# Feed-forward weights by two units in one DMA: 8 KB from each partition in place of 4 KB

## The reference

```
D_MODEL, SEQ, DEPTH, D_FF = 1024, 256, 2, 2816
# first_block, at the end of each of its 2 layers i
hn = rms_norm(h, norm_ffn[i])
gu = hn @ w_gate_up[i]                                  # 1024 x 5632
h = h + (jax.nn.silu(gu[..., :D_FF]) * gu[..., D_FF:]) @ w_down[i]
# second_block
cs = jax.nn.silu(c)
mod = cs @ w_ada[l] + b_ada[l]                          # w_ada: 1024 x 6144
# peer_ffn: rows of two tables of 16384 x 1024 by index
u = expert_u[idx]
v = expert_v[idx]
```

## Time and profile before

| | us |
|---|---|
| median of 3 timed runs | 1472.59 |
| lowest and highest | 1466.71, 1474.99 |
| the profiled execution's own time | 1478.32 |
| its span | 1476.7 |
| TensorE busy | 1384.1 (94%) |
| DVE busy | 1151.5 (78%) |
| ScalarE busy | 761.3 (52%) |
| GpSimd busy | 499.6 (34%) |

### The profile page before, as it was taken

One profiled execution on the slowest core, in us unless ns is written; L12 is line 12 of the kernel. 1 busy time (PEld: TensorE's weight loads), 2 busy tenths in 40 slices (PEclk: granted clock), 3 DMA queues, 4 the chain that ended last, 5 costly groups with the idle time before them and its releaser, 6 DMA issues.

```text
span 1476.7 us, 25782 instructions
## 1 busy us (share of the span) xinstructions
PE 1384.1 (94%) x8444; PEld 1072.0 (73%) x8444; DVE 1151.5 (78%) x2775; ACT 761.3 (52%) x1774; POOL 499.6 (34%) x600
## 2 busy tenths in 40 slices
PE   9999999999999899999999989989999988888888
PEld 9888999999889899998998985444454433333333
DVE  7767788778868688668799778877887888787764
ACT  6646444456556344456885544444444454444433
POOL 1011111110110111011110025766767666667672
PEclk9999999999999999999999999999999999999999
DMA  9999999999999999999999858999999999999997
GB/s 349 342 345 338 372 407 394 382 389 340 319 335 353 396 360 400 393 392 355 341 325 332 327 185 320 389 391 376 409 407 403 400 411 409 396 389 410 403 408 312
DMA packets 141598, 542.73 MB, mean 368 GB/s; under 512 B 22654, under 2 KB 22798, under 8 KB 128064
## 3 DMA queue, kind: packets, MB, share of 16 engines
q0 software_dynamic: 101904, 396.41, 72.3%
q1 hardware_dynamic: 39024, 142.44, 25.4%
q10 hardware_dynamic: 576, 2.72, 0.5%
HBM read 576.08 MB, written 135.27 MB: 482 GB/s over the span
## 4 chain that ended last, share of the span: by engine, by line
PE 53%; DMA 23%; DVE 11%; issue 5%; ACT 4%; POOL 3%; POOLq 0%; DVEq 0%; ACTq 0%; SPq 0%
DMA late<-expert_uv,idx 9%; PE PS L742 8%; PE PS L759 8%; PE PS L750 8%; PE PS L1263 7%; DMA attn<-expert_uv,idx 7%; DMA ada<-w_ada 6%; PE PS L893 3%; PE PS L790 3%; PE PS L1002 2%; PE PS L1006 2%; PE PS L1007 2%; DVE late L2563 2%; PE PS L1219 2%; DVE attn L2563 2%
## 5 line engine op out<-in xcount | busy, mean ns | idle before, releaser
L1366 ACT ACTIVATE early_splits<-ring 128x1024 fp32r<-128x1024 f32 x166 | 175.3, 1057 | 123.0 <-PE PS L750 87.5
L1825 DVE TENSOR_TENSOR early_splits<-ring,early_splits 128x1024 fp32r<-128x1024 f32 x166 | 202.6, 1221 | 33.5 <-ACT early_splits L1366 33.4
L2563 DVE CUSTOM_DVE_ANT_0 late<-late,PS 128x1024 f32<-128x1024 f32 x125 | 152.0, 1216 | 63.7 <-DMA late<-expert_uv,idx 63.0
L1727 ACT ACTIVATE gel<-dot 128x1 f32<-128x1 f32 x256 | 51.7, 202 | 278.7 <-DVE dot L2563 278.0
L2563 DVE CUSTOM_DVE_ANT_0 attn<-attn,PS 128x1024 f32<-128x1024 f32 x125 | 151.9, 1215 | 35.8 <-DMA attn<-expert_uv,idx 30.4
L1263 PE MATMUL PS<-late,wrg 128*128 128x512 f32 x284 | 136.4, 609 | 17.9 <-ACT wrg L1720 17.9
L1263 PE MATMUL PS<-attn,wrg 128*128 128x512 f32 x288 | 134.9, 601 | 7.4 <-ACT wrg L1720 6.5
L1300 PE MATMUL PS<-late,wrg 128*128 128x512 f32 x208 | 104.1, 626 | 31.2 <-ACT wrg L1720 31.2
L674 POOL DMA_INDIRECT attn<-expert_u,idx x93 | 87.8, 944 | 102.8 <-DVE idx L2515 74.7
L684 POOL DMA_INDIRECT attn<-expert_v,idx_v x93 | 93.0, 1000 | 78.2 <-DVE idx_v L2577 30.4
L1263 PEld LDWEIGHTS PS<-late,wrg 128*128 128x128 f32 x284 | 52.1, 193 | 86.9 <-issue 86.8
(11 more groups left out here) (458 smaller groups left out, 3379.7 us busy)
## 6 DMA issues: line engine op xcount, KB each, us to landing
ring<-wstream SPq DMA_DIRECT2D x257, 512.0 KB, 9.5
expert_uv<-expert_u POOLq DMA_DIRECT2D x64, 1024.0 KB, 14.4
expert_uv<-expert_v POOLq DMA_DIRECT2D x64, 1024.0 KB, 16.3
ada<-w_ada POOLq DMA_DIRECT2D x32, 512.0 KB, 13.5
late<-w_ada POOLq DMA_DIRECT2D x16, 512.0 KB, 14.9
late<-wstream SPq DMA_DIRECT2D x4, 512.0 KB, 8.8
attn<-expert_u,idx POOLq DMA_INDIRECT x93, 8.4
attn<-expert_v,idx_v POOLq DMA_INDIRECT x93, 7.7
```

The lines of the kernel that those rows point to most:

```text
L1366: act.activation(hi_of(u), raw(u), ACT.Copy).then_inc(hi_ready, 1)
L1825: ve.tensor_tensor(lo_of(u), raw(u), hi_of(u).bitcast(F32), ALU.subtract).then_inc(units_begun, 1)
L2563: ve.tensor_tensor_reduce(row, row, H2N[n // 8], 1.0, 0.0, ALU.mult, ALU.add, dot[:, n % 2, k:k + 1]).then_inc(dot_ready, 1)
```

## The change

Of the 66 feed-forward units of a layer, the 64 from an even one on (34 to 97 and 132 to 195) are loaded by twos. One DMA takes both units of a pair, 8 KB from each partition, into two neighbouring slots of the ring, and adds 16 to the semaphore of the even slot alone. It waits until both slots are free. The first and the last feed-forward unit of each layer (33 and 98, 131 and 196) and all other units are loaded as before. Who waits for an odd unit of a pair waits for the even slot's semaphore; the counts of the odd slots' semaphores leave the pairs out. The layout in memory is the same.

```
+PAIRED_FROM = [34, 132]
+PAIRED = 64
+        def paired(u):
+            return any(at <= u < at + PAIRED for at in PAIRED_FROM)
+        def landed(u):
+            if paired(u):
+                u -= u % 2
+            if u % 2:
+                return unit_landed[u % RING], 16 * sum(not paired(v) for v in range(u % RING, u + 1, RING))
+            return unit_landed[u % RING], 16 * (u // RING + 1)
@@ SyncE
+            def load_pair(u, i=None):
+                src = wstream[u // DMAU] if i is None else wstream[bass.ds(i * (RING // DMAU) + u // DMAU, 1)].rearrange(
+                    "o p e -> (o p) e")
+                sp.dma_start(ring[:, (u % RING) * D:(u % RING + 2) * D], src).then_inc(unit_landed[u % RING], 16)
-                with sp.Fori(0, 3 * NF // RING) as i:
-                    for m in range(RING):
-                        sp.wait_ge(units_begun, i * RING + (at + m - RING + 1))
-                        load(at + m, at + m, i)
+                for u in range(at, PAIRED_FROM[layer]):
+                    sp.wait_ge(units_begun, u - RING + 1)
+                    load(u, u)
+                at = PAIRED_FROM[layer]
+                with sp.Fori(0, PAIRED // RING) as i:
+                    for m in range(0, RING, 2):
+                        sp.wait_ge(units_begun, i * RING + (at + m - RING + 2))
+                        load_pair(at + m, i)
+                for u in range(at + PAIRED // RING * RING, at + PAIRED, 2):
+                    sp.wait_ge(units_begun, u - RING + 2)
+                    load_pair(u)
+                for u in range(at + PAIRED, LAYER_AT[layer] + PROJ_UNITS[layer] + 3 * NF):
+                    sp.wait_ge(units_begun, u - RING + 1)
+                    load(u, u)
@@ TensorE, slot_of and query
-                pe.wait_ge(unit_landed[u % RING], 16 * (u // RING + 1))
+                pe.wait_ge(*landed(u))
@@ ScalarE, split_hi
-                v = 16 * (u // RING + 1)
-                act.wait_ge(unit_landed[u % RING], v if i is None else i * 16 + v)
+                done, v = landed(u)
+                act.wait_ge(done, v if i is None else i * 16 + v)
```

## The result

On the chip of the first comparison the changed kernel took 1477.88 us in the median of 15 runs (1471.66 to 1488.28), the kernel before 1469.08 in that of 16 (1464.16 to 1474.99): ratio 1.006, 95% interval 1.0041 to 1.0078. A further run of the changed kernel, at 2248.72 us with a granted clock of 0.556, was disturbed and is left out. The forecast was 3.3 us less, from 1472.6 to 1469.3, and no change that could be told; measured are 8.8 us more. The time itself lies inside the forecast range of 1462.5 to 1483, which owes something to luck: the three runs that the forecast started from had their median 3.5 us above that of all 16. The profiled execution took 1485.47 us.

The account below looks back on a forecast made before the run. TensorE was taken to set the feed-forward pace, with DMA transfers having nothing to spare. From the three-run median 1472.6 us: 0 (SyncE) + 0 (ring) - 1.5 - 1.8 = -3.3, giving 1469.3; range 1462.5 to 1483.

Parts of the forecast that it names:

- SyncE at 0: SyncE's load issues: 64 fewer issues save nothing, and the added wait for one more split costs nothing; 0 us.
- The ring's latency: Ring loads in the feed-forward stages: a pair's least latency goes from 6.6 to 7.8 us, typically about 8 to 9.
- The ring's margin: Even unit of a pair, request to ScalarE's use: 10.0 us at the tightest, 12.5 at stage start, so 0 us.
- The `w_ada` rows at -3.3: Software queue, feed-forward stages: `w_ada` rows land earlier, so fewer DVE and TensorE stalls; 1.5 plus 1.8 us gained.
- The part of stage 0: First feed-forward stretch: 1.5 of 2.0 us of TensorE stalls behind late `w_ada` rows gained.
- The part of stage 1: Second feed-forward stretch: 1.8 of the 4.2 us TensorE stall gained, the lowered clock's 2.1 us left.
- All of it goes: Rival, feed-forward stages: rows land in time throughout and TensorE never stands; -8.3 us, 1464.3; 16%.
- The ring is late: Rival, ring loads: queues share by bytes or 8 KB reads are slower, pairs come late; 1488.6 us; 8%.
- a cover of 1.8 us: ScalarE's waits for the ring: those of up to 1.8 us were hidden, so longer ones would cost time.
- Starve: Rival, software queue: bursts of 8 KB packets delay `w_ada` rows in most of 15 cycles; 1482 to 1491 us; 10%.
- the packet is cut: Rival, hardware queue: 8 KB packets become two of 4 KB, only the later issue is left; 1475.6 us; 6%.

Follow-up runs that it names:

- f0: The changed kernel run again, on another chip, against the kernel before: ratio 1.0077 (1.0053 to 1.01).
- f2: The changed kernel with DVE's sums of `w_ada` rows moved behind the third split, in both loops: ratio to the kernel before 1.0016, 8.9 us less than f0.
- e1: The changed kernel with pairs only from the seventh unit of each stage on (40 and 138), none at a stage start: ratio to the kernel before 1.0025.
- e2: The changed kernel with only the first three pairs of each stage, the other units loaded singly: ratio to the kernel before 1.0028.
- e4: As e1, with the middle pair of each six-unit cycle loaded as two single units: ratio to the kernel before 0.9972, and 0.9998 when run again.
- f1: The changed kernel with ScalarE taking unit 34's (132's) coarse half behind the last chunks of normed input: ratio to the kernel before 1.0018, 7.4 us less than f0.
- g1: The changed kernel with the moves of both f1 and f2: ratio to the kernel before 0.9988 (0.9968 to 1.0008).
- g2: The kernel of e4 with the move of f2 added: ratio to the kernel before 0.9998 (0.9983 to 1.0013).
- g3: The kernel before against itself, unchanged, for a second profile: ratio 1.0009 (0.9993 to 1.0024).

## Why the prediction was wrong

- **SyncE at 0.** Right as to issuing: no wait in either trace is put down to it. But the wait that SyncE got, for one split more, is what makes the request late.
- **The ring's latency.** The least of 7.8 us was right to the tenth in the first stage (6.4 in the second); "about 8 to 9" for the typical pair was not: 10.1 in the median, 11.6 for the first pair. In f0 it was 9.1 and 9.7 in the two stages. The transfer was priced at 3.8 us, and some 4.0 us ahead of it (6.6 - 2.6) were taken over from the quickest single load. In 170 to 240 us q1's packets show a pair's first one 3.6 to 5.4 us after the issue in the changed kernel and 1.0 to 3.9 in f2. "A pair is asked for every 5.7 us, so the ring hardly queues behind itself" can't hold at 10.1 us: nearly two are under way.
- **The ring's margin: the step that failed.** "Against the margin of 10.0 us I take 0 for the ring", and at the stage's start a pair of 8 to 9 us and ScalarE's 1.06 us were to fit into 12.5: neither was so. For the steady cycle I took 10.0 us from one place. Over the cycles of that trace the tight pair has as little as 8.9 (units 84 and 90). For the stage start I measured to DVE. But ScalarE does not take the unit just before DVE. Its rows in the trace before:

```profile
452.31 1.06 ACT L1366 ACTIVATE early_splits<-ring 128x1024 fp32r<-128x1024 f32 x1 [0.70 <-PE PS L893]
453.28 0.49 ACT L1496 ACTIVATE x_split<-X,col 128x256 fp32r<-128x256 f32 x1
```

  From 444.3 to 452.31 are 8.0 us, and what follows on ScalarE is the normed input. I had asked what is queued behind the added wait on SyncE, and not behind ScalarE's wait, which the change makes longer. The ring was worth about +9 us and not 0; e1, e2, e4, f1 and f2 show its two parts. The prediction also read ScalarE's waits for the ring before from two of the three buffers, 9.0 us in six and 1.8 at most; with the third it was 13.7 us in nine, the longest 2.0, and all were hidden.
- **The `w_ada` rows at -3.3.** In the two profiles it held: the rows land in 12.7 us in place of 14.1, and DVE's 5.9 + 4.8 us of waits are gone. The part of stage 0, 1.5 us, is borne out further: both profiles of the kernel before lose 2.4 us there, f2 and g1 nothing; single late rows still came in e1, f1 and g2. The part of stage 1 is not: the forecast took it off the median of the runs, and g3 lacks the 4.2 us event. The 5.7 us by which the profiled execution lay above the median match what g3 lacks there (6.5 us), so I seem to have counted that event twice: once by carrying the difference over, once as a gain.
- **The rivals.** "All of it goes" came true as to the rows, and the time still rose. "The ring is late" named the right place, but by equal bytes, at 16 us, and at 8%; its mechanism is out (packets turn about), its sign was right. I gave it a size from a cover of 1.8 us. In the changed kernel the eight waits of 2.6 to 3.6 us in stage 0 gave gaps of 1.07 us at most, and the one of 4.42 us at its start 2.93. "Starve" and "the packet is cut" are out.

The rule weighed there, at least 1 MiB in a DMA for the highest bandwidth (the Trainium skill, "DMA: Bandwidth & Descriptors", "Rules for kernel authors"), gave nothing here: the DMA share is full before and after, 1.00 to 1.02, and g1, whose pairs cost nothing that shows, is at 0.9988 with 1 inside the interval.

**Left open.** f1 and f2 alone leave 0.18% and 0.16%, together 0.34%, while the changed kernel has 0.60% (0.41 to 0.78) and 0.77% (0.53 to 1.0) on two chips. f0 had six runs, and a part of a profile varies by up to 6.5 us between two executions of one kernel; of the 8.9 us between f0 and f2 the traces show 4.7 in the two stages. Why a pair's first packet comes later when the cycle is late was not tested, nor why the cycle of stage 0 recovers in f0 and not in the first profile.

## What to carry to other kernels

Merging two transfers into one moves the first one's request to the second one's: before doing it, take the margin from request to use at the first engine that waits, over all cycles and at each stage's start, and compare it with the landing under load. Then read on that engine what stands behind the wait; moving a split behind urgent work (f1), or work that nobody wants yet out from ahead of the split that frees the buffer (f2), each gave back about 8 us here. And take a second profile before a single stall enters a sum: if the profile lies above the median of the runs, the stall may be all of the difference.

## What the runs showed of the hardware

- A transfer's latency depended on when it was asked for: with the sums of `w_ada` rows (2.9 us) out of the way of the request (f2), pairs landed in 8.2 us in the median of stage 0 and 8.7 of stage 1, against 9.1 and 9.7 in f0 on the same chip, at the same bytes and nearly the same share (1.00 in both stretches of f2, 1.00 and 0.99 in f0).
- Gaps of TensorE of 1.98, 0.32 and 0.63 us within 4 us were followed, from the third on, by 3.4 us at a granted clock of 0.50. In f0 2.21 and 0.44 us went with 6.8 us at 0.50 (from 144.3), and single gaps of 2.64 us (e1) and 2.21 (f1), just before 190 us, with 3.4 us each. Gaps of 0.57, 0.32 and 0.64 us (f0, 460 to 466 us) left the clock at 1.00, and so did the steady gaps of at most 1.07 us, no more than one a cycle: 283 to 288 us, behind the gap of 0.89, is at 1.00.
